# Input tables of a state-space branch made by GpSimd in the feed-forward stage, inputs in one transfer per half, output tables in three buffers

## The reference

```
dt = exp(log_dt);  mag = exp(lr*dt)                  # 64 groups, 64 states each
abar = mag * (cos(li*dt) + i sin(li*dt));  f = (abar - 1) / (lr + i li)
bbar = f * b                                         # (64 groups, 64 states, 16 inputs)
s_t = abar * s_(t-1) + bbar * u_t
y_t = Re(c * s_t) + d * u_t                          # c: (64 groups, 16 outputs, 64 states)
```

## Time and profile before

| | us |
|---|---|
| median of 3 runs | 1914.26 (1912.48 to 1914.29) |
| the profiled execution | 1908.86 |
| its span, first to last instruction | 1907.1 |
| TensorE busy (matmul) | 1815.8 (95%) |
| VectorE busy | 1041.0 (55%) |
| ScalarE busy | 899.2 (47%) |
| GpSimd busy | 203.7 (11%) |
| chain of waits that ended last | TensorE 65%, VectorE 13%, ScalarE 8%, DMA 4% |

### The profile page before, as it was taken

One profiled execution on the slowest core, in us unless ns is written; L12 is line 12 of the kernel. 1 busy time (PEld: TensorE's weight loads), 2 busy tenths in 40 slices (PEclk: granted clock), 3 DMA queues, 4 the chain that ended last, 5 costly groups with the idle time before them and its releaser, 6 DMA issues.

```text
span 1907.1 us, 31670 instructions
## 1 busy us (share of the span) xinstructions
PE 1815.8 (95%) x12181; PEld 1622.0 (85%) x12181; DVE 1041.0 (55%) x1612; ACT 899.2 (47%) x1190; POOL 203.7 (11%) x362
## 2 busy tenths in 40 slices
PE   6899999999999998999999998799999999899996
PEld 6899999999999998899998877688777777788885
DVE  3455555555433346655453337887477677645442
ACT  4666666666533343333332223255555655633332
POOL 0011111111000010710004750100000000000001
PEclk9999999999999996999999997899999999999998
DMA  3222222222122352232324423944211221233432
GB/s 116 89 71 69 70 78 77 77 88 71 58 93 88 96 166 82 80 98 88 99 88 129 135 101 118 265 126 118 73 62 61 78 68 53 77 100 99 134 98 99
DMA packets 71443, 182.84 MB, mean 96 GB/s; under 512 B 22916, under 2 KB 23108, under 8 KB 71240
## 3 DMA queue, kind: packets, MB, share of 16 engines
q1 hardware_dynamic: 68824, 172.89, 29.6%
q0 software_dynamic: 2544, 8.91, 1.3%
HBM read 162.62 MB, written 16.80 MB: 94 GB/s over the span
## 4 chain that ended last, share of the span: by engine, by line
PE 65%; DVE 13%; ACT 8%; issue 7%; DMA 4%; SPq 1%; POOL 1%; ACTq 0%; DVEq 0%
PE J L808 25%; PE J L1066 14%; PE J L820 6%; PE J L1037 6%; DMA WR<-weights 3%; PE Z L858 2%; DVE WL L1776 2%; PE J L1237 1%; DVE C L2005 1%; POOL E L2460 1%; ACT E L1389 1%; ACT E L1385 1%; SPq L721 1%; PE Z L912 1%; ACT WH L1317 1%
## 5 line engine op out<-in xcount | busy, mean ns | idle before, releaser
L1776 DVE TENSOR_TENSOR WL<-WR,WH 128x1024 fp32r<-128x1024 f32 x271 | 343.7, 1269 | 294.7 <-ACT WH L1317 285.5
L1317 ACT ACTIVATE WH<-WR 128x1024 fp32r<-128x1024 f32 x271 | 285.4, 1054 | 229.9 <-DMA WR<-weights 101.8
L808 PE MATMUL J<-XH,WH 128*128 128x264 f32 (+1 forms) x1376 | 285.8, 289 | 14.3 <-DVE XL L1780 6.6
L808 PE MATMUL J<-XL,WH 128*128 128x264 f32 (+1 forms) x1376 | 280.8, 286 | 0.0
L808 PE MATMUL J<-XH,WL 128*128 128x264 f32 (+1 forms) x1376 | 280.6, 286 | 0.0
L808 PEld LDWEIGHTS J<-XH,WH 128*128 128x128 f32 x1376 | 216.7, 191 | 20.2 <-issue 8.1
L808 PEld LDWEIGHTS J<-XL,WH 128*128 128x128 f32 x1376 | 215.8, 191 | 0.0
L808 PEld LDWEIGHTS J<-XH,WL 128*128 128x128 f32 x1376 | 215.0, 191 | 0.0
L2460 POOL TENSOR_SCALAR_AFFINE_SELECT E<-E 128x128 f32<-128x128 f32 (+1 forms) x160 | 51.8, 360 | 447.0 <-DVE E L1858 239.4
L1066 PE MATMUL J<-X2H,WH 128*128 128x512 f32 x168 | 70.7, 421 | 9.1 <-DVEq L2191 5.1
L2478 POOL TENSOR_TENSOR SA<-SQ 128x512 f32<-128x512 f32 (+1 forms) x3 | 3.9, 1298 | 695.4 <-ACT SQ L1562 503.8
(11 more groups left out here) (445 smaller groups left out, 4228.0 us busy)
## 6 DMA issues: line engine op xcount, KB each, us to landing
WR<-weights SPq DMA_DIRECT2D x271, 512.0 KB, 3.6
cp_dram<-CQR POOLq DMA_DIRECT2D x8, 288.0 KB, 2.4
cp_dram<-CQI POOLq DMA_DIRECT2D x8, 288.0 KB, 2.4
CPR<-cp_dram SPq DMA_DIRECT2D x8, 288.0 KB, 4.0
CPI<-cp_dram SPq DMA_DIRECT2D x8, 288.0 KB, 4.3
X<-tokens SPq DMA_DIRECT2D x4, 528.0 KB, 5.7
H<-tokens SPq DMA_DIRECT2D x8, 264.0 KB, 3.8
res_dram<-H SPq DMA_DIRECT2D x1, 2048.0 KB, 8.0
```

The source lines that it names most:

```text
L808: mm = pe.matmul(o[:, 512 * h:512 * h + half], ws[:, s, w], xs[:, a:a + half], start=(k == 0 and i == 0), stop=(k == 7 and i == 2))
L1317: act.activation(WH[:, n % SPLIT, :], WR[:, n % RAW, :], ACT.Copy).then_inc(w_hi, 1)
L1776: dve.tensor_tensor(WL[:, n % SPLIT, :], WR[:, n % RAW, :], WH[:, n % SPLIT, :].bitcast(F32), ALU.subtract).then_inc(w_lo, 1)
```

## The change

GpSimd takes over BB and all eight input tables. They now stand in the upper part of the feed-forward stage's own memory (FH from its ninth tile on), right after GpSimd's last sum of the w_out stage, and all go to DRAM (`bb_dram`, `bp_dram`); ScalarE waits after its eighth feed-forward tile until they are stored. Scan tables follow them. The matrix BM is loaded at the beginning of the w_out stage. In the second block BB is loaded back, BP has two buffers and CP three. The order of (input, position) within a table and in US is swapped, so that US of a half is one transfer and TK's rows are written with a stride of eight partitions. VectorE's parameters 4 to 6 become 3 to 5. `states_in(0)` moves in front of the last u job, which takes a later slot turn, `kernel_out(0)` and `states(0)` move with it; GpSimd clears TK.

```diff
 def t_u(m):
+    return T_U + m if m < DT - 1 else T_SSM + 1
 def t_zs(m):
-    return T_SSM + 2 + 3 * m if m else T_SSM
+    return T_SSM + 2 + 3 * m
 def t_turned(m):
-    return T_SSM + 3 * m if m else T_SSM + 1
+    return T_SSM + 3 * m if m else T_SSM - 1
...
+        place, _ = places(U[5], U[3] + FT * SEQ * 4)
+        RVR, RVI, BQR[2], BQI[2] = ...
+        BQ_ALIVE = (U[4] - U[3]) // (SEQ * 4)
+        assert BQ_ALIVE == 8
...
@@ SyncE, w_out stage
                 sp.dma_start(H[:, m * L1:(m + 1) * L1], x_view[:, m]).then_inc(h_landed, 16)
+                if m == 0:
+                    sp.dma_start(BM[:], bmat).then_inc(mat_landed, 16)
@@ SyncE, u stage
             def load_us(half):
-                src = u_dram.rearrange("(g p) j c -> j p g c", p=GP)
-                for j in range(SUB):
-                    sp.dma_start(US[j * GP:(j + 1) * GP, g], src[j][:, g]).then_inc(us_landed[half], 16)
+                src = u_dram.rearrange("(g p) j c -> (p j) g c", p=GP)
+                sp.dma_start(US[:, g], src[:, g]).then_inc(us_landed[half], 16)
             for m in range(3, DT):
                 load_one(N_U + m)
                 if m >= 4:
                     store_u(m - 4)
-            for x in range(2):
-                sp.wait_ge(cq_stored[x], 16 * DT)
-            for m in range(2):
-                load_cp(m)
+                if m == 4:
+                    sp.wait_ge(bb_stored, 32)
+                    (BBR, BBI from bb_dram)
+                if m in (5, 6):
+                    (waits for bq_stored and cq_stored)
+                    load_bp(m - 5)
+                    load_cp(m - 5)
+                if m == 7:
+                    load_cp(2)
             for k in range(4):
                 load_one(N_SSM + k)
-                store_u(4 + k)
                 if k == 0:
                     load_us(0)
-            load_us(1)
+                store_u(4 + k)
-            load_bp(1)
             load_kernel(0)
+            load_us(1)
             for m in range(DT):
                 if N_SSM + 4 + m < N_ATT:
                     load_one(N_SSM + 4 + m)
-                if m >= 1 and m + 1 < DT:
-                    sp.wait_ge(y_done, m)
-                    load_cp(m + 1)
-                if m + 2 < DT:
-                    load_bp(m + 2)
+                if m + 2 < DT:
+                    sp.wait_ge(bt_turned, m + 1)
+                    load_bp(m + 2)
+                if m >= 1 and m + 2 < DT:
+                    sp.wait_ge(y_done, m)
+                    load_cp(m + 2)
                 if m + 1 < DT:
                     load_kernel(m + 1)
@@ TensorE
-            for m in range(DT):
-                job2(N_U + m, T_U + m, X2H, X2L, xl_ready if m == 0 else None, 2 * DT)
+            for m in range(DT - 1):
+                job2(N_U + m, t_u(m), X2H, X2L, xl_ready if m == 0 else None, 2 * DT)
+            states_in(0)
+            job2(N_U + DT - 1, t_u(DT - 1), X2H, X2L)
             for m in range(DT):
                 job2(N_SSM + m, t_zs(m), X2H, X2L)
-                if m == 0:
-                    states_in(0)
-                else:
+                if m:
                     turn_y(m - 1)
@@ ScalarE, feed-forward
-            repeat(act, FT, 2, up)
+            repeat(act, BQ_ALIVE, 2, up)
+            act.wait_ge(bq_ready, DT)
+            for k in range(2):
+                act.wait_ge(bq_stored[k], 16 * DT)
+            act.wait_ge(bb_stored, 32)
+            repeat(act, FT - BQ_ALIVE, 2, lambda i: up(i + BQ_ALIVE))
@@ ScalarE, u stage
+            for m in range(DT):
+                if m == DT - 1:
+                    kernel_out(0)
                 split_hi(N_U + 3 + m)
@@ VectorE, u stage: BB, RVR, RVI, inputs(m) and the clearing of TK taken out
+                if m == DT - 2:
+                    states(0)
@@ GpSimd, after gather_squares(Q_MIX) and the wait for pow_ready
-            pool.wait_ge(xl_ready, 2 * DT)
+            pool.wait_ge(mat_landed, 16)
+            wide = [P, PAIRS, GP]
+            turned(BQ[0][:], BQ[1][:], FR.., FI.., BM[:, 0], BM[:, 1], C1[:], C2[:])
+            for j in range(SUB):
+                pool.tensor_copy(RVR[:, :, j], PWR[:, :, SUB - 1 - j])
+                link(pool.tensor_copy(RVI[:, :, j], PWI[:, :, SUB - 1 - j]))
+            for x in range(2):
+                pool.dma_start(bb_dram[x], ...).then_inc(bb_stored, 16)
+            def inputs(m):
+                if m >= 2:
+                    pool.wait_ge(bq_stored[m % 2], 32 * (m // 2))
+                link(tt(k1, bbr, rr))
+                link(tt(k2, bbi, ri))
+                link(tt(BQR[m % 2][:], k1, k2, ALU.subtract))
+                pool.dma_start(bp_dram[m, 0], ...).then_inc(bq_stored[m % 2], 16)
+                link(tt(k1, bbr, ri))
+                link(tt(k2, bbi, rr))
+                tt(BQI[m % 2][:], k1, k2, ALU.add).then_inc(bq_ready, 1)
+                pool.wait_ge(bq_ready, m + 1)
+                pool.dma_start(bp_dram[m, 1], ...).then_inc(bq_stored[m % 2], 16)
+            for m in range(DT):
+                inputs(m)
```

More of the change, by code:

```diff
@@ L351, in build @@
         TS = place("TS", [P, 2, 4 * PAIRS])
+        BM = place("BM", [P, 2, PAIRS, GP])
+        C1 = place("C1", [P, PAIRS, GP])
+        C2 = place("C2", [P, PAIRS, GP])
+        BQ = [place(f"BQ{x}", [P, PAIRS, GP]) for x in range(2)]
+        place, _ = places(U[5], U[3] + FT * SEQ * 4)
+        RVR = place("RVR", [P, PAIRS, SUB])
+        RVI = place("RVI", [P, PAIRS, SUB])
+        BQR = [place(f"BQR{k}", [P, PT_, GP, SUB]) for k in range(2)]
+        BQI = [place(f"BQI{k}", [P, PT_, GP, SUB]) for k in range(2)]
+        BQ_ALIVE = (U[4] - U[3]) // (SEQ * 4)
+        assert BQ_ALIVE == 8
         place, _ = places(M1 + 8480, M1 + 8480 + 4 * L1)
@@ L369, in build @@
         BBI = place("BBI", [P, PAIRS, GP])
[L370 to L374, removed]
         YT = place("YT", [P, SUB, PT_, GP])
         DD = place("DD", [P, GROUPS, GP])
-        CPR = [place(f"CPR{k}", [P, PT_, SUB + 1, GP]) for k in range(2)]
-        CPI = [place(f"CPI{k}", [P, PT_, SUB + 1, GP]) for k in range(2)]
+        CPR = [place(f"CPR{k}", [P, PT_, SUB + 1, GP]) for k in range(3)]
+        CPI = [place(f"CPI{k}", [P, PT_, SUB + 1, GP]) for k in range(3)]
         GS = place("GS", [GP, GT * P])
-        BQR = [place(f"BQR{k}", [P, PT_, SUB, GP]) for k in range(2)]
-        BQI = [place(f"BQI{k}", [P, PT_, SUB, GP]) for k in range(2)]
+        BPR = [BPR, place("BPR1", [P, PT_, GP, SUB])]
+        BPI = [BPI, place("BPI1", [P, PT_, GP, SUB])]
         place, at7 = places(M1, M2)
@@ L2046, in parameters @@
                     link(dve.tensor_scalar(NUM[:], ABR[:], 1.0, None, ALU.subtract))
-                if part == 4:
+                if part == 3:
                     mul(PT1[:], NUM[:], are)
@@ L2212, in _ @@
-            inputs(DT - 1)
-            for k in range(2):
-                dve.wait_ge(u_stored[k], 16 * DT // 2)
-            dve.memset(TK[1][:], 0.0).then_inc(tk_zeroed, 1)
             def states(m):
@@ L2568, in _ @@
                     gather_one(Q_FFN, m, SA1, SEQ)
-            for m in range(1, DT):
-                pool.wait_ge(bq_ready, m + 1)
-                for x, src in enumerate((BQR[m % 2], BQI[m % 2])):
-                    pool.dma_start(bp_dram[m, x], src[:].rearrange("p a j q -> p (a j q)")).then_inc(bq_stored[m % 2], 16)
+            pool.wait_ge(h_ready, 2 * DT)
+            pool.memset(TK[0][:], 0.0).then_inc(tk_zeroed, 1)
+            for k in range(2):
+                pool.wait_ge(u_stored[k], 16 * DT // 2)
+            pool.memset(TK[1][:], 0.0).then_inc(tk_zeroed, 1)
             pool.wait_ge(yt_turned, DT)
```

147 lines of the change are left out of this document (66 added, 81 removed).

## The result

The changed kernel takes 1893.5 us (median of four executions, 1891.4 to 1894.4) where the kernel before took 1914.3 beside it: ratio 0.9885 [0.9864, 0.9906]. Another sample of the same kernel gave 1892.7, ratio 0.9898 [0.9883, 0.9913]. The forecast was 1902.3 us in a range from 1895 to 1912: the sign was right, the size was not, 20.8 us gained instead of 12.0 (by the two intervals 17 to 26).

What follows compares the result with a forecast made beforehand. It took one bad stretch, 1192.4 to 1245.0 us, rooted in VectorE's input tables, as the bound. 14.0 + 2.1 + 1.0 - 4.6 - 0.5 = 12.0 us off the median 1914.3 gave 1902.3, range 1895 to 1912.

Steps and rivals of the forecast that it cites:

- Output tables, 2.1 us: State-space loop: three buffers remove the waits for output tables CPI; gain 2.1 us (1.5 to 2.1).
- Parameters, 1.0 us: End of w_out: one VectorE power step moves a tile earlier, delaying a weight load less; gain 1.0 us (0 to 1.5).
- GpSimd beside VectorE, -4.6 and -0.5: Norm before feed-forward: GpSimd's products delay VectorE, costing 4.6 us in the eight CT/XL pairs and 0.5 in the chain before.
- GpSimd's own time, 826 to 841 for the last table: From w_out's end into feed-forward: GpSimd makes BB and eight input tables, finishing at 826 to 841 us.
- Feed-forward loop 0, gate 0: Feed-forward: VectorE's slower operations cost 0, and ScalarE's wait for the stored tables after its eighth tile costs 0.
- The u stage, gain 14.0: Second block, u jobs to first outputs y: removing the waits recovers 14.0 of 19.0 us lost (7 to 19).
- I take 5.0 left of the 19.0: At states_in(0): weights late behind US leave 3.7 us idle and some 1.3 at half clock; bounds 0 and 12.
- The first rival: US load: the single transfer is quick, in before weights need DMA engines; 5 us more gain, 1897; chance 0.15.
- Its reason against: US load: argument against a quick single transfer, that pieces stay at 256 bytes and their number stays.
- Their root is VectorE: Bad stretch of the second block: 54 VectorE table operations of 0.69 us queue with slot releases and weights, causing the losses.
- Profile to median: Whole kernel: profiled execution 1908.9 us, so about 1896.9 after; the median is 5.4 above it, so 1902.3.

Runs made afterwards that it cites:

- e2: Changed kernel with two buffers instead of three for the output tables CP, loaded only after the outputs of the tile before: 1900.4 us, ratio 0.9937.
- e3: Changed kernel, GpSimd pausing after tile 0's tables until VectorE's last XL pair is done, then making the other seven: 1888.6 us, ratio 0.9876.
- e6: Changed kernel with all of GpSimd's tables, BB included, made only after VectorE's last XL pair: 1900.8 us, ratio 0.9941.
- e1: Changed kernel with each half of US loaded by eight transfers of 16 partitions again: 1903.3 us, ratio 0.9944.
- e16: Changed kernel plus 14 stores of 256 KB each, issued by GpSimd from the BB tables to unused DRAM: 1900.2 us, ratio 0.9924.
- e7: Changed kernel with each half of US in eight transfers, each over all 128 partitions: 1892.0 us, ratio 0.9887.
- e12: Kernel before, with one wide transfer per half of US and four of six VectorE operations per input table left out: 1903.7 us, ratio 0.9950.
- e15: Kernel before, one wide transfer per US half, four of six VectorE operations per input table left out, table stores cut to an eighth: 1897.5 us.
- e4: Changed kernel with states_in(0), its PSUM slots, kernel_out(0) and states(0) back behind the first z job: 1896.9 us, ratio 0.9918.
- a0: Changed kernel run once more, nothing edited: 1892.7 us, ratio 0.9898 against the kernel before.

## Why the prediction was wrong in size, by its own steps

- *Output tables, 2.1 us*: the loop shrank by 2.5 us (97.9 to 95.4). Right; e2 adds that with two buffers the changed kernel is 7.7 us slower.
- *Parameters, 1.0 us*: the first CT of the norm comes at 737.32 instead of 738.28. The number fits, but it isn't shown: over the profiles of all runs this time lies between 737.4 and 741.4 with the old order and between 735.6 and 741.4 with the new one, and no run undoes this part alone.
- *GpSimd beside VectorE, -4.6 and -0.5*: -4.2 and -0.1 (20.1 to 20.2). Near, and e3 and e6 show the cause. That it is so near is partly luck: the pairs themselves lost 3.3 us, and 0.9 came with the long split behind them, which the working didn't have.
- *GpSimd's own time, 826 to 841 for the last table*: 827.7, the end of its last issue. *Feed-forward loop 0, gate 0*: TensorE is busy in 91.30 of 91.30 us though VectorE rose from 46.8 to 68.0, and e6 shows that the gate costs once GpSimd is 45 us later. Right.
- *The u stage, gain 14.0*: 18.7 (52.65 to 33.95). **This is the step that failed: "I take 5.0 left of the 19.0"; 0.3 were left** (33.95 us against the clean 33.6), and this term holds 4.7 of the 5.9 us by which the parts exceed the forecast. US itself ran as forecast: it landed 8.5 us after its issue, where the working had 9.3. Wrong was what stands behind it. The working let the weights go out when US was in and land 6 us later, with the hold of SyncE and the landing time taken from rows of eight narrow transfers in full queues; the 126 GB/s were the rate of all transfers in 2 us, not that of US.

  With the single wide one the weights were issued 6.76 us after US, 1.7 us before it landed, and landed in 4.4. Put on one axis (the u stage starts 3.4 us later here) US was issued 0.8 us later and the weights landed 3.4 us sooner than forecast, and the slot was free at 1207.58, just as TensorE came to it: the pause of 3.7 us and the slow stretch behind it didn't happen. e1, with eight narrow transfers, had the pause (3.10) just where I put it; e16, with the stores back, had it too (3.2). The first rival had the outcome (nothing left, 5 us more) and 0.15, but not the way to it: US was not in before the weights asked for the DMA engines. Its reason against, that the pieces stay at 256 bytes, doesn't hold between narrow and wide: e7 has the same pieces and loses nothing.
- *"Their root is VectorE"*: this sentence carried the 14.0 and was wrong as a cause, though the sum didn't show it. VectorE was one of three; lightened alone it wins 0.4 us, taken last of the three 12.7. The rows pointed past it: a DMA share of 0.96 and a split that waited 6.91 us for weights were read as an echo of VectorE.
- *Profile to median*: 17.7 us of span became 20.8 of medians. The profile of before happened to be a quick execution (5.4 below the median), that of after less so (2.1), 3.3 us that no step contains. Without them the gain would have been 17.5 instead of 20.8, still 5.5 over the forecast.

In sum 18.7 + 2.5 + 1.0 - 4.2 - 0.1 = 17.9, against 17.7 in the spans. How the stretch got from "VectorE, transfers" to the changed kernel can be read from the time between the first u job and the first outputs y in the profiles: 74.2 us in e12, 66.1 with the stores cut as well (e15), 65.5 in the changed kernel with the old place of `states_in(0)` (e4), 62.8 in the changed kernel. So the stores carry about 8 and the new place about 3 (and 1.7 more in the round behind it); what is left for the earlier loads of BP and CP is under 1, each read from a single profile. Left open: why the next issue is held 5.14 us behind a single one, and what the parameters' new place is worth.

## What to carry to other kernels

When a stretch has a full queue, a full engine and late weights at once, lighten each alone and in pairs before calling one the root: here three changes that win 0.4, 1.7 and 4.4 us alone win 18.4 together, and taken back singly they cost 8.8 to 12.7. Ask too what the lightened engine sets off sooner: a quicker VectorE brought its stores forward into the transfers of US. Take the durations for a new form of transfer from rows of its own form or bound them from both sides in earnest; a narrow transfer's rows say little about a wide one. GpSimd's products cost nothing beside the VectorE operations here that read PSUM and one tile of SBUF (0.76 us with and without them), and 0.1 to 1.0 us each beside those with two SBUF inputs on the critical chain; a pause over that chain won 4.2 us.

## What the runs showed of the hardware that was not expected

- Eight transfers of 16 partitions took 5.7 us each to land and held SyncE for 8.3 (e1), eight of 128 partitions with the same bytes took 3.3 and 4.9 (e7); the step between them is 10 us of kernel time. Over all profiles the first half of US took 13.0 to 17.4 us in narrow transfers and 7.4 to 11.9 in wide ones.
- Behind a single issue of 0.77 us for 1 MB in 256-byte pieces the next one on the queue took 5.14 us (4.36 in a0, 7.45 in e12).
- Lightening VectorE in the kernel before made the wait for bp_dram longer (6.2 to 10.8 us) with the time unchanged.
